# Seven-product feed-forward turns: two down units in every turn, a tail of short and long units, and low-half terms last in the first turn

## The chip, the core and the metric

The kernel runs on one NeuronCore of a Trainium2 chip. The metric is the device time of one execution in microseconds (us). TensorE (PE in the profile) multiplies, VectorE (DVE), ScalarE (ACT) and GpSimd (POOL) prepare its operands and take its results, and SyncE (SP) issues the weight loads.

## The reference

Two transformer-like blocks are computed on 528 tokens (16 learned ones and 512 inputs; the last stages keep only 512). The first has two layers, each with a feed-forward part, a mixer and a second feed-forward part; the second block has one layer and ends in a feed-forward part. What matters here is the feed-forward part:

```python
def swiglu(x, w_gu, w_down):
    gate, up = jnp.split(x @ w_gu, 2, axis=-1)
    return (jax.nn.silu(gate) * up) @ w_down
...
        h = h + 0.5 * swiglu(rms_norm(h, ffn1_norm[l]), ffn1_w_gu[l], ffn1_w_down[l])
...
        h = h + 0.5 * swiglu(rms_norm(h, ffn2_norm[l]), ffn2_w_gu[l], ffn2_w_down[l])
...
        x = x + (jax.nn.silu(h2 @ w_ffn_gate[l]) * (h2 @ w_ffn_up[l])) @ w_ffn_down[l]
```

Rows of `x` have 1024 numbers (8 tiles of 128, `KD`) and the hidden width is 2816 (22 tiles, `FT`). All of it is float32.

## The kernel before, in words

**Numbers in two halves.** Each float32 operand is held as a high part (`xh`, `wh`, `ah`) and a low part (`xl`, `wl`, `al`), and a product is the sum of three terms: high by high, low tokens by high weights, high tokens by low weights. For weights, ACT writes `wh` from the loaded `raw` (`hi`, line 1312) and POOL writes `wl = raw - wh` (`split`, line 586; `split_half`, line 598, for one half of a unit). A term with `wl` can't start before POOL is done.

**Units.** PE works through a list of units, one 128-column block of a weight matrix each, with 2 to 8 row tiles. Unit k uses slot k mod 4 of `raw`, `wh` and `wl`. SP loads unit k once PE has finished unit k-4. Results of plain units go to PSUM `pair[k mod 2]`; PE may start unit k only when the result of unit k-2 has been read (the semaphore `evacuated`).

**Feed-forward stages.** Four of the five feed-forward parts run in the form `ffn_w`. They are called A (layer 0, first), B (layer 0, second), C (layer 1, first) and D (second block, 512 tokens) here. Each computes 4 hidden tiles with plain units (8 units) and the other 18 in 18 **turns**, t = 0 to 17. A turn computes gate and up of one hidden tile with seven products (a Strassen-like scheme with combined weights `SH`/`SL` and combined tokens `TH`/`TL`) of 12 matmuls each, into the four banks of `aux`. In the code a turn is `turn` in each engine's block; the products are issued by `product` (line 790). DVE adds the products up (lines 1940, 1948, 1951, 1956), ACT applies silu, and DVE ends the tile by writing its low part `al` (line 1924), which raises `a_ready`.

**Down units.** The down projection needs finished hidden tiles. Inside a turn, after the fourth and after the last product, PE runs a down unit with four row tiles (`BLOCK`, 24 matmuls at 528 tokens) of an earlier group of hidden tiles; DVE adds its result to `hT` (`add_residual`, line 1848). `DOWNS` says how many a turn has: 2 in turns 0 to 14, 1 in turns 15 and 16, none in turn 17; that is 32 units, 4 groups by 8 column blocks. After a turn without its second down unit the next turn's first product would need `aux` bank 3 at once, so turns 16 and 17 put it into a bank of `pair` (`own_pair`, `first_bank`), and turn 17 moves its gate product one place later.

**The tail.** After turn 17 come 8 down units of six row tiles (`W_TAIL`, hidden tiles 16 to 21; 36 matmuls each), m = 0 to 7. Units 0 and 1 are interleaved by row tile (with one matmul group of each last), because hidden tile 21 comes late. In stages A, B and C the result of each tail unit goes through `residual`: DVE adds it to `hT` (line 1848), ACT squares it and writes `xh` (lines 1325, 1326), then `wh` of unit m+3 (line 1312), and DVE adds the square up and writes `xl` (lines 1837, 1838), all before DVE turns to the next unit's result. The next stage's first unit uses `xh`/`xl` row tile by row tile, and its sum of squares (line 759) needs all eight. In stage D the tail only stores: DVE adds, ACT issues the output DMA (line 1469), and the kernel ends.

Of the kernel before, what the change touches and what calls it, by code (L numbers as in the profile page):

```python
# [27 lines left out]
P = 128  # L28
# [3 lines left out]
KD = D // P  # L32
# [24 lines left out]
PLAIN = 4  # L57
# [79 lines left out]
def build(nc, a, out):  # L137
    with ExitStack() as ctx:
# [209 lines left out]
        def singles():  # L348

            k, m = W_FIRST + 4 * 12, 0  # L350
            for t in range(12, W_PAIRS):
                yield t, k, range(m, m + DOWNS[t])
                k, m = k + 2 + DOWNS[t], m + DOWNS[t]

# [128 lines left out]
        def _(sp):  # L483
# [29 lines left out]
            def ffn_w(l, ub, gate, up, down, up0, hold=False):  # L513
# [7 lines left out]
                for g in range(1, 4):  # L521
# [6 lines left out]
                for t, k, ms in singles():  # L528
                    load(l, ub + k, cols(up, l, 0, KD, up0 + (PLAIN + t) * P), KD)
                    load(l, ub + k + 1, cols(gate, l, 0, KD, (PLAIN + t) * P), KD)  # L530
                    for j, m in enumerate(ms):
                        load(l, ub + k + 2 + j, cols(down, l, 3 * BLOCK, BLOCK, m * P), BLOCK)
# [41 lines left out]
        def _(pool):  # L574
# [34 lines left out]
            def ffn_w(l, ub, fs):  # L609
# [3 lines left out]
                for g in range(1, 4):  # L613
# [4 lines left out]
                run(l, ub + W_END, [W_TAIL] * 4, KD // 4)  # L618
# [88 lines left out]
        def _(pe):  # L707
# [63 lines left out]
            def turn(l, k, n, i, fs, th, xs, a0, nd=2, own=None):  # L771
# [12 lines left out]

                def product(b, w, x, lo=None):
                    for t, (u, y) in enumerate(((w[0], x[0]), (w[0], x[1]), (w[1], x[0]))):
                        if t == 2 and lo is not None:
                            pe.wait_ge(*lo)
                        for kk in range(4):
                            mm = nc.tensor.matmul(b[:, 0:th], u(kk), y(kk), start=t == 0 and kk == 0, stop=t == 2 and kk == 3)  # L790
                    return mm
                up, gate = (wh[:, s, :], wl[:, s, :]), (wh[:, s1, :], wl[:, s1, :])

                pe.wait_ge(S["split_hi"], U(l, k, i) + 1)
                if own is not None:
                    pe.wait_ge(S["evacuated"], U(l, k - 1) + 1 + PAIRS)
                else:
                    pe.wait_ge(S["w_free"], n + 1)
                product(first_bank(own), weights(*up, 0), tokens(0, 0), (S["split_done"], U(l, k, i) + 1)).then_inc(S["w_prod"], 1)
                if own is not None:  # L800
                    pe.wait_ge(S["w_up"], n * 2 - 1)
                product(aux[:, 2, :], weights(*up, HK4), tokens(4, 0)).then_inc(S["gemm_done"], 1)
                pe.wait_ge(S["w_tlo"], 4 * fs + 4)

                def gate_product():
                    pe.wait_ge(S["split_hi"], U(l, k + 1, i) + 1)
                    product(aux[:, 0, :], weights(*gate, HK4), combined(3), (S["split_done"], U(l, k + 1, i) + 1)).then_inc(S["gemm_done"], 1)
# [4 lines left out]
                if nd:  # L812
                    gemm(l, k + 2, BLOCK, xs, th, i, ready=lambda kk: (S["a_ready"], a0))
                else:
                    gate_product()
# [6 lines left out]
                if own is not None:  # L822
                    pe.wait_ge(S["w_free"], n + 1)
                product(aux[:, 3, :], weights(SH, SL, 1536), tokens(4, 1)).then_inc(S["w_prod"], 1)
                if nd > 1:
                    gemm(l, k + 3, BLOCK, xs, th, i)

            def ffn_w(l, ub, fi, x0, T, nrm, fs):
# [13 lines left out]
                for g in range(1, 4):  # L842
                    with pe.Fori(0, 4) as i:
                        turn(l, ub + W_FIRST + 16 * (g - 1), n0 + 4 * (g - 1) + i, i, fs, th, *block(g - 1))
                for t, k, ms in singles():
                    turn(l, ub + k, n0 + t, 0, fs, th, *block(3), len(ms), own_pair(t, ub))
# [7 lines left out]
                for j in range(2, KD):  # L854
                    gemm(l, k + j, W_TAIL, (ah, al), th)
# [444 lines left out]
        def _(act):  # L1300
# [62 lines left out]
            def turn(l, k, n, i, T, f, tile, nd=2, after=2, own=None):  # L1363

                th = T // 2
                if own is not None:
                    act.wait_ge(S["w_read"], n * 2 - 1)
                act.wait_ge(S["w_prod"], n * 5 + 5 + 1)
                nc.scalar.activation(tm(SQA)[:, 0:th], first_bank(own)[:, 0:th], ACT.Copy).then_inc(S["w_p1"], 1)
                if nd > 1:  # L1370
                    hi(l, k + 3, i, BLOCK * P)
                q = k + 2 + nd
                if after is None:
                    hi(l, q + 1, i, W_TAIL * P)
# [9 lines left out]
                if after is not None:  # L1384
                    hi(l, q + 2, i, (BLOCK if after else W_TAIL) * P)
# [1334 lines left out]
```

## Time and profile before

| what | value |
|---|---|
| median of 3 runs | 3198.28 us (3195.89 to 3201.35) |
| the profiled execution's own time | 3201.69 us |
| its span (first to last instruction in the trace) | 3199.9 us |
| PE busy | 3111.8 us, 97% of the span |
| PE weight loads busy | 2848.1 us, 89% |
| DVE, ACT, POOL busy | 67%, 38%, 42% |
| mean granted TensorE clock | 0.989 of full |

The engine rows give the time in which an engine had an instruction under way. A matmul that waits in PE's pipe counts as busy, so that short gaps of PE don't show in the 97%; starts of consecutive groups show them. A row of the windows view gives a stretch of the trace and its length, then the busy time and the instructions of PE, PE's weight loads, DVE, ACT and POOL, then the mean TensorE clock that was granted (1.00 is full speed), the DMA share and GB/s. A row of the timeline gives start, duration, engine, line, operation, output and inputs, shape and count, and in brackets the idle time before it and what ended it.

### The profile page before, as it was taken

Reading aid. Unit: us, or ns where it says so; the run is one execution under the profiler, and the core shown is the slowest. Engines: PE = TensorE matmul, PEld = TensorE weight load, DVE = VectorE, ACT = ScalarE, POOL = GpSimd, SP = SyncE. Lnnn points to the kernel's source line nnn. Section 1 sums busy time; section 2 is a strip of 40 time slices with the busy share of each in tenths; the row PEclk is TensorE's granted clock in tenths of the full one; section 3 lists DMA queues with packets and bytes.
Section 4 is the critical chain, followed back from the end, with each engine's and each line's share of the span. In section 5 each row is a group of like instructions: output and inputs, shape, how many; then the busy total and the mean of one; then the engine's idle time right before and its main releaser. Section 6 shows DMA issues by size and latency. Waiting matters only on the chain.

```text
span 3199.9 us, 56181 instructions
## 1 busy us (share of the span) xinstructions
PE 3111.8 (97%) x21236; PEld 2848.1 (89%) x21236; DVE 2140.2 (67%) x3071; ACT 1214.0 (38%) x1825; POOL 1353.5 (42%) x960
## 2 busy tenths in 40 slices
PE   8999999999999999999999999999999998999999
PEld 7999988899999999999998888788888786788998
DVE  7888663477588886888763467633234578768885
ACT  5433443322343444444344322332324344344442
POOL 3444442233534444444443233644455563344443
PEclk9999999999999999999999999999999999999999
DMA  4333322233323333333332123333333534233333
GB/s 134 98 95 93 90 74 60 51 90 121 99 86 97 97 104 88 88 97 99 91 82 71 47 79 126 100 97 106 93 97 87 112 97 135 66 95 97 100 101 96
DMA packets 546214, 299.02 MB, mean 93 GB/s; under 512 B 24368, under 2 KB 529840, under 8 KB 545904
## 3 DMA queue, kind: packets, MB, share of 16 engines
q1 hardware_dynamic: 515728, 259.86, 28.7%
q10 hardware_dynamic: 30304, 36.65, 3.6%
q8 instruction: 125, 2.05, 0.3%
q14 instruction: 57, 0.47, 0.0%
HBM read 278.37 MB, written 16.91 MB: 92 GB/s over the span
## 4 chain that ended last, share of the span: by engine, by line
PE 59%; issue 22%; POOL 8%; DVE 7%; DMA 1%; ACT 1%; ACTq 1%; POOLq 0%; DVEq 0%; SPq 0%
PE aux L790 21%; PE pair L725 21%; PE pair L727 15%; POOL wl L586 8%; DMA raw<-ffn_w_gu 1%; DVE R L1909 1%; DVE tmp L1919 1%; ACTq L1702 0%; DVE al L1924 0%; DVE TL L1915 0%; DVE hT L1848 0%; DMA raw<-w_ffn_gate 0%; DVE R L1908 0%; DVE xl L2152 0%; DVE tmp L1824 0%
## 5 line engine op out<-in xcount | busy, mean ns | idle before, releaser
L586 POOL TENSOR_TENSOR wl<-raw,wh 128x256 fp32r<-128x256 f32 (+3 forms) x848 | 1174.8, 1405 | 1816.7 <-ACT wh L1312 1368.6
L1312 ACT ACTIVATE wh<-raw 128x1024 fp32r<-128x1024 f32 (+4 forms) x613 | 511.5, 835 | 481.8 <-DMA raw<-ffn_w_gu 250.5
L1848 DVE SCALAR_TENSOR_TENSOR hT<-pair,hT 128x528 f32 (+3 forms) x208 | 144.7, 695 | 170.7 <-PE pair L725 127.2
L727 PE MATMUL pair<-xh,wh 128*128 128x264 f32 x1344 | 233.6, 296 | 22.5 <-DVE xl L2152 11.1
L725 PE MATMUL pair<-xh,wh 128*128 128x512 f32 x776 | 220.7, 406 | 0.1
L727 PE MATMUL pair<-xl,wh 128*128 128x264 f32 x1344 | 220.7, 286 | 0.0
L727 PEld LDWEIGHTS pair<-xh,wh 128*128 128x128 f32 x1344 | 190.0, 193 | 30.0 <-issue 14.8
L727 PE MATMUL pair<-ah,wh 128*128 128x264 f32 x1256 | 211.8, 286 | 4.9 <-ACT wh L1312 2.9
L727 PE MATMUL pair<-xh,wl 128*128 128x264 f32 x1344 | 215.3, 286 | 0.8 <-POOL wl L586 0.8
L725 PE MATMUL pair<-xl,wh 128*128 128x512 f32 x776 | 212.3, 395 | 0.0
L725 PE MATMUL pair<-xh,wl 128*128 128x512 f32 x776 | 209.2, 395 | 0.3 <-POOL wl L586 0.3
L727 PE MATMUL pair<-al,wh 128*128 128x264 f32 x1256 | 208.9, 283 | 0.0
L727 PE MATMUL pair<-ah,wl 128*128 128x264 f32 x1256 | 191.3, 283 | 0.0
L727 PEld LDWEIGHTS pair<-xl,wh 128*128 128x128 f32 x1344 | 187.6, 190 | 0.1
L727 PEld LDWEIGHTS pair<-xh,wl 128*128 128x128 f32 x1344 | 184.8, 190 | 1.2 <-POOL wl L586 1.2
L727 PEld LDWEIGHTS pair<-ah,wh 128*128 128x128 f32 x1256 | 176.2, 188 | 7.2 <-ACT wh L1312 3.3
L1360 ACT ACTIVATE ah<-tmp 128x528 f32 (+3 forms) x110 | 70.5, 641 | 289.2 <-DVE tmp L1919 289.2
L725 PEld LDWEIGHTS pair<-xh,wh 128*128 128x128 f32 x776 | 145.0, 190 | 36.6 <-issue 4.7
L725 PEld LDWEIGHTS pair<-xh,wl 128*128 128x128 f32 x776 | 146.1, 188 | 34.8 <-POOL wl L586 0.7
L725 PEld LDWEIGHTS pair<-xl,wh 128*128 128x128 f32 x776 | 146.6, 189 | 33.1 <-issue 0.2
L727 PEld LDWEIGHTS pair<-al,wh 128*128 128x128 f32 x1256 | 175.3, 188 | 0.0
L727 PEld LDWEIGHTS pair<-ah,wl 128*128 128x128 f32 x1256 | 168.2, 188 | 0.0
(429 smaller groups left out, 6671.8 us busy)
## 6 DMA issues: line engine op xcount, KB each, us to landing
raw<-ffn_w_gu SPq DMA_DIRECT2D x176, 512.0 KB, 3.9
raw<-w_in SPq DMA_DIRECT2D x103, 512.0 KB, 3.9
raw<-ffn_w_down SPq DMA_DIRECT2D x96, 256.0 KB, 2.8
raw<-ffn_w_down SPq DMA_DIRECT2D x32, 384.0 KB, 3.4
raw<-w_out SPq DMA_DIRECT2D x24, 512.0 KB, 3.8
raw<-w_ffn_gate SPq DMA_DIRECT2D x22, 512.0 KB, 4.6
raw<-w_ffn_up SPq DMA_DIRECT2D x22, 512.0 KB, 3.8
gate_scratch<-gst ACTq DMA_DIRECT2D x32, 256.0 KB, 3.1
```

The lines of the kernel that those rows point to most:

```text
L586: ins = nc.gpsimd.tensor_tensor(wl[:, k % SPL, n], raw[:, k % SPL, n], wh[:, k % SPL, n].bitcast(F32), ALU.subtract)
L725: return nc.tensor.matmul(pp[:, 0, :], wk, x[:, kk, t0:t0 + SEQ], start=first, stop=last)
L727: mm = nc.tensor.matmul(pp[:, h, 0:th], wk, x[:, kk, t0 + h * th:t0 + (h + 1) * th], start=first, stop=last)
L790: mm = nc.tensor.matmul(b[:, 0:th], u(kk), y(kk), start=t == 0 and kk == 0, stop=t == 2 and kk == 3)
L1312: nc.scalar.activation(wh[:, k % SPL, n0:n], raw[:, k % SPL, n0:n], ACT.Copy).then_inc(S["split_hi"], 1)
L1360: nc.scalar.activation(ah[:, bass.ds(tile, 1), 0:T].rearrange("p o t -> p (o t)"), tm(A32, T), ACT.Copy).then_inc(S["ahi_done"], 1)
L1848: v.scalar_tensor_tensor(halves(hm, T // 2), psum_pair(k, T // 2), factor, halves(hm, T // 2), ALU.mult, ALU.add).then_inc(S["evacuated"], ...
L1909: step(v.scalar_tensor_tensor(t2, b22, own(kk + 4), t1, ALU.mult, ALU.subtract))
L1919: v.tensor_tensor(tm(A32, T), tm(SG, T), tm(US, T), ALU.mult).then_inc(S["a_done"], 1)
```

## The change

**Down units.** All 18 turns have two down units of four row tiles. The four that are new (in turns 16 and 17) take hidden tiles 16 to 19 for the column blocks m = 2, 4, 6 and 7. Their tail units keep only hidden tiles 20 and 21: two row tiles, 12 matmuls at 528 tokens. The tail is then long, long, short, long, short, long, short, short. The number of matmuls is the same. `own_pair`, `first_bank` and the moved gate product are gone, and turns 12 to 15 are a loop. Each stage has 88 units where it had 84.

**The first turn.** In turn 0 PE issues the two terms with `wh` of its first three products, and only then the terms with `wl` of the three, in order.

```diff
-DOWNS = (2,) * 15 + (1, 1, 0)
-assert len(DOWNS) == W_PAIRS and sum(DOWNS) == 4 * KD
-W_KT = [KD] * (2 * PLAIN) + [x for nd in DOWNS for x in [KD, KD] + [BLOCK] * nd] + [W_TAIL] * KD
+TAIL_SHORT = (2, 4, 6, 7)
+TAIL_KT = tuple(W_TAIL - BLOCK if m in TAIL_SHORT else W_TAIL for m in range(KD))
+W_KT = [KD] * (2 * PLAIN) + [KD, KD, BLOCK, BLOCK] * W_PAIRS + list(TAIL_KT)
...
-                k = ub + W_END
-                with sp.Fori(0, KD // 4) as i:
-                    for j in range(4):
-                        load(l, k + j, cols(down, l, 4 * BLOCK, W_TAIL, j * P + i * (4 * P)), W_TAIL, i)
+                for m, kt in enumerate(TAIL_KT):
+                    load(l, ub + W_END + m, cols(down, l, FT - kt, kt, m * P), kt)
...
+                up_lo, gate_lo = (S["split_done"], U(l, k, i) + 1), (S["split_done"], U(l, k + 1, i) + 1)
 
                 pe.wait_ge(S["split_hi"], U(l, k, i) + 1)
-                if own is not None:
-                    pe.wait_ge(S["evacuated"], U(l, k - 1) + 1 + PAIRS)
+                pe.wait_ge(S["w_free"], n + 1)
+                if first:
+                    main(*p1)
+                    main(*p2)
+                    pe.wait_ge(S["w_tlo"], 4 * fs + 4)
+                    pe.wait_ge(S["split_hi"], U(l, k + 1, i) + 1)
+                    main(*p4)
+                    pe.wait_ge(*up_lo)
+                    rest(*p1).then_inc(S["w_prod"], 1)
+                    rest(*p2).then_inc(S["gemm_done"], 1)
+                    pe.wait_ge(*gate_lo)
+                    rest(*p4).then_inc(S["gemm_done"], 1)
                 else:
...
-                if nd:
-                    gemm(l, k + 2, BLOCK, xs, th, i, ready=lambda kk: (S["a_ready"], a0))
-                else:
-                    gate_product()
+                gemm(l, k + 2, BLOCK, xs, th, i, ready=lambda kk: (S["a_ready"], a0))
...
-                if nd > 1:
-                    gemm(l, k + 3, BLOCK, xs, th, i)
+                gemm(l, k + 3, BLOCK, xs, th, i)
...
                 for j in range(2, KD):
-                    gemm(l, k + j, W_TAIL, (ah, al), th)
+                    o = W_TAIL - TAIL_KT[j]
+                    gemm(l, k + j, TAIL_KT[j], (ah[:, o:W_TAIL, :], al[:, o:W_TAIL, :]), th)
```

Here `main` issues a product's two terms with high weights (line 777 of the changed kernel) and `rest` the term with low weights (line 781). The order of instructions on PE at the head of stage A's turn 0, before:

```order
L790 MATMUL aux<-xh,wh 128x264 x4
L790 MATMUL aux<-xl,wh 128x264 x4
L790 MATMUL aux<-xh,wl 128x264 x4
L790 MATMUL aux<-xh,wh 128x264 x4
L790 MATMUL aux<-xl,wh 128x264 x4
L790 MATMUL aux<-xh,wl 128x264 x4
```

And with the change:

```order
L777 MATMUL aux<-xh,wh 128x264 x4
L777 MATMUL aux<-xl,wh 128x264 x4
L777 MATMUL aux<-xh,wh 128x264 x4
L777 MATMUL aux<-xl,wh 128x264 x4
L777 MATMUL aux<-TH,wh 128x264 x4
L777 MATMUL aux<-TL,wh 128x264 x4
L781 MATMUL aux<-xh,wl 128x264 x8
L781 MATMUL aux<-TH,wl 128x264 x4
L777 MATMUL aux<-TH,SH 128x264 x4
```

The first group with `wl` moved behind 24 matmuls where 8 stood before it. On PE from the middle of stage A's tail into the next stage (units 2 and 3, before):

```order
L727 MATMUL pair<-ah,wh 128x264 x12
L727 MATMUL pair<-al,wh 128x264 x12
L727 MATMUL pair<-ah,wl 128x264 x12
L727 MATMUL pair<-ah,wh 128x264 x12
L727 MATMUL pair<-al,wh 128x264 x12
```

And with the change units 5, 6 and 7 and the head of the next stage (`xh` appears):

```order
L716 MATMUL pair<-ah,wh 128x264 x12
L716 MATMUL pair<-al,wh 128x264 x12
L716 MATMUL pair<-ah,wl 128x264 x12
L716 MATMUL pair<-ah,wh 128x264 x4
L716 MATMUL pair<-al,wh 128x264 x4
L716 MATMUL pair<-ah,wl 128x264 x4
L716 MATMUL pair<-ah,wh 128x264 x4
L716 MATMUL pair<-al,wh 128x264 x4
L716 MATMUL pair<-ah,wl 128x264 x4
L716 MATMUL pair<-xh,wh 128x264 x2
```

Units 6 and 7 have 12 matmuls each where they had 36; ACT, POOL and DVE keep one piece of work for each unit between them, and only its `wh` and `wl` get shorter.

## Rows read from the trace of the kernel before

**Rows 1.** Waits of PE: us in total, times, longest, for two causes.

```profile
PE aux L790 <- POOL wl L586: 9.1, 4, 2.8
PE aux L790 <- DVE tmp L1940: 7.3, 4, 1.9
```

**Rows 2.** Timeline, turn 0 of stage B: start, us, engine, work, [idle before].

```profile
921.03 0.65 PE L790 MATMUL aux<-xh,wh 128*128 128x264 f32 x4
...
923.02 0.61 ACT L1312 ACTIVATE wh<-raw 128x512 fp32r<-128x512 f32 x1
923.98 2.27 POOL L598 TENSOR_TENSOR wl<-raw,wh 128x512 fp32r<-128x512 f32 x1
924.07 0.76 PE L790 MATMUL aux<-xh,wl 128*128 128x264 f32 x4 [1.91 <-POOL wl L586]
...
927.87 0.69 DVE L1924 TENSOR_TENSOR al<-tmp,ah 128x528 fp32r<-128x528 f32 x1
...
930.57 0.40 PE L727 MATMUL pair<-ah,wh 128*128 128x264 f32 x2
```

**Rows 3.** Windows from `al`'s end to turn 0's first down unit (A, C, D).

```profile
74.90:75.38 0.48, 0.48 (x6) 0.48 (x5) 0.00 (x0) 0.24 (x1) 0.48 (x1) 1.00 1.14 346
1297.40:1299.43 2.03, 2.03 (x18) 2.03 (x17) 0.00 (x0) 0.23 (x1) 2.03 (x2) 0.99 0.87 242
2891.46:2893.36 1.90, 1.90 (x18) 1.90 (x17) 0.00 (x0) 0.23 (x1) 1.90 (x2) 1.00 0.92 269
```

**Rows 4.** Windows: a turn with two down units, at 528 and 512 tokens.

```profile
299.98:316.00 16.02, 16.02 (x134) 16.02 (x133) 13.95 (x17) 6.47 (x10) 7.19 (x5) 1.00 0.35 99
3107.24:3122.80 15.56, 15.56 (x110) 14.51 (x110) 14.00 (x17) 6.58 (x10) 7.32 (x5) 1.00 0.35 102
```

**Rows 5.** Windows from turn 15's start to the tail's start; stages A to D.

```profile
316.00:356.43 40.43, 38.48 (x302) 38.06 (x301) 32.11 (x40) 14.72 (x21) 17.18 (x10) 0.96 0.35 99
1167.17:1206.39 39.22, 36.94 (x302) 36.52 (x301) 32.50 (x39) 14.94 (x21) 17.18 (x10) 1.00 0.35 102
1535.10:1575.55 40.45, 38.48 (x302) 38.06 (x301) 31.95 (x39) 14.73 (x22) 17.22 (x10) 0.96 0.34 99
3122.80:3162.67 39.87, 37.30 (x277) 35.83 (x276) 32.05 (x39) 14.74 (x21) 17.21 (x10) 0.96 0.35 99
```

**Rows 6.** Windows of three stretches behind a wait of PE (the seventh number: TensorE clock).

```profile
352.00:355.30 3.30, 3.30 (x18) 3.30 (x17) 0.43 (x1) 0.00 (x0) 1.23 (x1) 0.50 0.02 5
925.30:928.50 3.20, 3.20 (x18) 3.20 (x17) 3.17 (x4) 1.66 (x4) 1.36 (x2) 0.51 0.04 10
1202.00:1206.00 4.00, 4.00 (x33) 4.00 (x34) 0.78 (x2) 0.00 (x0) 2.75 (x2) 1.00 0.33 97
```

**Rows 7.** Timeline, stage A's tail: DVE and PE, to the sum of squares.

```profile
364.67 0.71 DVE L1848 SCALAR_TENSOR_TENSOR hT<-pair,hT 128x528 f32<-128x528 f32 x1 [4.29 <-PE pair L727]
365.52 1.69 PE L727 MATMUL pair<-ah,wh 128*128 128x264 f32 x12 [0.16 <-DVE hT L1848]
...
367.74 0.70 DVE L1848 SCALAR_TENSOR_TENSOR hT<-pair,hT 128x528 f32<-128x528 f32 x1
369.94 1.61 PE L727 MATMUL pair<-ah,wh 128*128 128x264 f32 x12
371.09 0.70 DVE L1848 SCALAR_TENSOR_TENSOR hT<-pair,hT 128x528 f32<-128x528 f32 x1
...
374.28 1.61 PE L727 MATMUL pair<-ah,wh 128*128 128x264 f32 x12
374.48 0.71 DVE L1848 SCALAR_TENSOR_TENSOR hT<-pair,hT 128x528 f32<-128x528 f32 x1
...
391.84 0.71 DVE L1848 SCALAR_TENSOR_TENSOR hT<-pair,hT 128x528 f32<-128x528 f32 x1 [0.91 <-PE pair L727]
394.51 0.76 DVE L1838 SCALAR_TENSOR_TENSOR xl<-hT,gcur,xh 128x528 fp32r<-128x528 f32 x1
...
396.76 1.05 PE L759 MATMUL aux<-tmp,con 128*128 128x264 f32 x4
```

More of the change, by code:

```diff
@@ L348, in singles @@
         def singles():
[L350 to L353, printed above, removed]
+            for t in range(16, W_PAIRS):
+                yield t, W_FIRST + 4 * t, TAIL_SHORT[2 * (t - 16):2 * (t - 16) + 2]
         class Plan:
@@ L520, in ffn_w @@
                     load(l, ub + 2 * j + 1, cols(up, l, 0, KD, up0 + j * P), KD)
-                for g in range(1, 4):
+                for g in range(1, 5):
                     k = ub + W_FIRST + 16 * (g - 1)
@@ L612, in ffn_w @@
                 n0 = W_PAIRS * fs
-                for g in range(1, 4):
+                for g in range(1, 5):
                     with pool.Fori(0, 4) as i:
@@ L617, in ffn_w @@
                     turn(l, ub + k, n0 + t, 0, len(ms))
-                run(l, ub + W_END, [W_TAIL] * 4, KD // 4)
+                for m, kt in enumerate(TAIL_KT):
+                    split(l, ub + W_END + m, kt)
             def ffn(l, ub, beside):
@@ L769, in norm_sum_2, with turn @@
                 mm.then_inc(S["ss_done"], 1)
-            def turn(l, k, n, i, fs, th, xs, a0, nd=2, own=None):
+            def turn(l, k, n, i, fs, th, xs, a0, first=False):
                 s, s1 = k % SPL, (k + 1) % SPL
@@ L783, in combined, with main @@
                     return [lambda kk, x=x: x[:, m, kk, :] for x in (wth(th), wtl(th))]
-                def product(b, w, x, lo=None):
[L786 to L791, printed above, removed]
+                def main(b, w, x):
+                    for t, y in enumerate(x):
+                        for kk in range(4):
+                            nc.tensor.matmul(b[:, 0:th], w[0](kk), y(kk), start=t == 0 and kk == 0, stop=False)
@@ L792, in turn, with rest @@
+                def rest(b, w, x):
+                    for kk in range(4):
+                        mm = nc.tensor.matmul(b[:, 0:th], w[1](kk), x[0](kk), start=False, stop=kk == 3)
+                    return mm
+                def product(b, w, x, lo=None):
+                    main(b, w, x)
+                    if lo is not None:
+                        pe.wait_ge(*lo)
+                    return rest(b, w, x)
                 up, gate = (wh[:, s, :], wl[:, s, :]), (wh[:, s1, :], wl[:, s1, :])
+                p1, p2, p4 = ((aux[:, 3, :], weights(*up, 0), tokens(0, 0)), (aux[:, 2, :], weights(*up, HK4), tokens(4, 0)),
+                              (aux[:, 0, :], weights(*gate, HK4), combined(3)))
@@ L802, in turn @@
-                product(aux[:, 2, :], weights(*up, HK4), tokens(4, 0)).then_inc(S["gemm_done"], 1)
-                pe.wait_ge(S["w_tlo"], 4 * fs + 4)
-                def gate_product():
+                pe.wait_ge(S["w_free"], n + 1)
[10 more added lines that the diff above has]
+                    rest(*p4).then_inc(S["gemm_done"], 1)
+                else:
+                    product(*p1, up_lo).then_inc(S["w_prod"], 1)
+                    product(*p2).then_inc(S["gemm_done"], 1)
@@ L806, in gate_product @@
                     pe.wait_ge(S["split_hi"], U(l, k + 1, i) + 1)
[L807 to L809 removed]
+                    product(*p4, gate_lo).then_inc(S["gemm_done"], 1)
                 pe.wait_ge(S["w_hi"], n * 2 + 1)
                 product(aux[:, 1, :], weights(SH, SL, 512), combined(1), (S["w_lo"], n * 2 + 1)).then_inc(S["w_prod"], 1)
[L812 to L815 removed]
+                gemm(l, k + 2, BLOCK, xs, th, i, ready=lambda kk: (S["a_ready"], a0))
@@ L841, in block @@
                     return (ah[:, o:o + BLOCK, :], al[:, o:o + BLOCK, :]), fi * FT + BLOCK * (g + 1)
-                for g in range(1, 4):
+                turn(l, ub + W_FIRST, n0, 0, fs, th, *block(0), first=True)
+                with pe.Fori(0, 3) as i:
+                    turn(l, ub + W_FIRST + 4, n0 + 1 + i, i, fs, th, *block(0))
+                for g in range(2, 5):
                     with pe.Fori(0, 4) as i:
@@ L1406, in ffn_w @@
                         w_his(n0, 1, n0 * 5 + 5)
-                for g in range(1, 4):
+                for g in range(1, 5):
                     with act.Fori(0, 4) as i:
@@ L1992, in ffn_w @@
                         w_sums(l, ub + W_FIRST, n0, 0)
-                for g in range(1, 4):
+                for g in range(1, 5):
                     with dve.Fori(0, 4) as i:
```

48 lines of the change are left out of this document (15 added, 33 removed).

## The prediction

> **What bounds the kernel now.** I read the waits of PE first, then the timeline of PE to see when equal pieces of work start, then windows. PE is busy for 97% of the span, and nearly all of the rest is a few waits, so time changes only where PE's waits or its clock change. Two kinds of wait lie where the edits are, once in each of the four feed-forward stages [rows 1]: turn 0 waits for POOL's `wl` (9.1 us in four waits, 2.3 each), and turn 17 waits for DVE's reading of `aux` (line 1940; 7.3 us in four, 1.8 each). The number of matmuls doesn't change. The questions are what stands behind each wait once it is gone, and whether the tail, with less PE work per unit, still keeps PE fed.
>
> **Part 1, the low-half terms of turn 0.** The reader should look at stage B [rows 2]. PE starts at 921.03, issues 8 matmuls, and at 922.0 stands until POOL's `wl` is there at 924.07. With the change it goes on with the high terms of the second product until 922.97 (a turn's 132 matmuls in 16.02 us [rows 4] give 0.121 us each, 0.97 for 8). The third product needs ACT's `wh` of the gate unit, which ends at 923.63; its 8 high matmuls end at 924.65. Eight low matmuls of the up unit: 925.6. The gate's `wl` ends at 926.25; four matmuls: 926.8. Product four (12 matmuls): 928.25. Then stands the down unit, which waits for `a_ready` of the last plain tile: 927.87 + 0.69 = 928.56. That chain on DVE and ACT doesn't hang on PE, so it doesn't move. PE starts the down unit at about 928.6 instead of 930.57: 1.97 us won. The end of `al` is thus the floor in every stage. It lies 0.48, 2.01, 2.03 and 1.90 us ahead of the down unit in A, B, C and D [rows 2, 3], less 0.05 each for waking: **-6.2 us**. The waits that take the old one's place (0.7 for `wh`, 0.7 for the gate's `wl`, 0.35 for `al`) make up most of the old one; in B, C and D a good part of the gain is instead the clock that fell behind the old wait [rows 6]. What moves with PE (SP's loads behind units k and k+1, DVE's reading behind product four) comes earlier, none of it later.
>
> **Part 2, turns 15 to 17.** A turn with two down units takes 16.02 us, at 512 tokens 15.56, with no wait inside [rows 4]. Three take 48.06 (D: 46.68). Before, the three took 40.43, 39.22, 40.45 and 39.87 us [rows 5], the waits and slow clocks of turn 17 included. So they get longer by 7.6, 8.8, 7.6 and 6.8: +30.9 us. Four down units of 24 matmuls are 4 x 24 x 0.121 = 11.6 us of work; what is missing to that (4.0 in A, 2.8 in B) is what the change wins at turn 17. I take no wait for turns 15 to 17: down units stand between the last product and the next first one as in turn 14.
>
> **Part 3, the tail of stages A, B and C.** Here the trace shows the change's price. One tail unit takes 374.28 less 369.94 = 4.34 us on PE [rows 7]; a short one takes a third, 1.45. But each unit, long or short, has the same chain behind it: DVE's addition 0.7, ACT's square and `xh`, DVE's square sum and `xl`, and only then the next addition. Units 0 and 1 end together, so DVE starts in arrears, and the reader can see its own pace: additions start at 364.67, 367.74, 371.09 and 374.48, that is 3.07, then 3.35 and 3.39 apart [rows 7]. That is less than 4.34, so PE doesn't wait now. It is far more than 1.45. And PE may begin unit m only when unit m-2 has been added. With starts A(m) of the additions at a pace of 3.38 behind the third, and 0.85 us from such a start to PE's (365.52 less 364.67 [rows 7]), in the times of stage A before:
>
> unit 2 runs 365.52 to 366.97; unit 3 waits for A(1) + 0.85 = 368.6, to 372.9; unit 4, to 374.4; unit 5 waits for A(3) + 0.85 = 375.3, to 379.7; unit 6, to 381.1; unit 7 waits for A(5) + 0.85 = 381.23 + 0.85 = 382.1, to 383.5; the next stage's first unit waits for A(6) + 0.85 = 385.5.
>
> A(7) is 388.0. From an addition's start to the end of its `xl` it is 394.51 + 0.76 - 391.84 = 3.43 [rows 7], so the sum of squares can start at 391.5. Before it started at 396.76. The tail is **5.3 us** shorter, where PE's work is 11.6 us shorter; five new waits (1.6, 0.9, 1.0, 1.9 and about 1.0 at the end) eat the rest. Three stages: -15.8 us.
>
> **Part 4, the tail of stage D.** There ACT only stores, and one DVE operation a unit follows. PE stays the bound: a long unit is about 4.2 us (4.34 by the ratio of 15.56 to 16.02), four short ones save 4 x 2.8 = 11.2. The last two outputs follow each other by 1.4 us instead of 4.2, for which I give 0.3 (bounds 0 and 1.4, all of the time between them): -10.9 us. The weights' loads: a short unit's is a third of the bytes, and the load of unit m waits for unit m-4 as before, two long units back at least; I cost it at nothing, hidden under these. Four more units a stage cost SP, ACT and POOL four more commands, under PE's 16 us turns.
>
> **Sum.** -6.2 + 30.9 - 15.8 - 10.9 = -2.0 us, if the clock stays at full speed at all the new waits.
>
> **The clock.** Behind a wait the granted clock is at times half (1.2 instead of 2.4 GHz): 0.50 for over 3 us behind turn 17's wait in stage A, 0.51 behind turn 0's in B; behind the same wait of 1.8 us in stage B's turn 17 it stayed at 1.00 [rows 6]. Such a fall costs 3.3 x 0.5 = 1.65 us of PE. The new tail has 2.9 us of waits in its last 6 us, and in turn 0 1.8 us are split into three. In the tail the falls that lie before the last two waits are hidden by them; one behind the wait before the next stage, or at the sum of squares, is not. In turn 0 about 0.6 to 1.1 is left of it, since the wait for `al` takes some. I take half of these: half of three tails at 1.7 and of four first turns at 0.9, 4.3 us. Bounds: none, and two falls in each tail with one in each turn 0, 3 x 3.3 + 4 x 1.1 = 14 us. The sum is then +2.3. The profiled execution took 3201.7, so its like would be 3204.0; the median is 3.4 lower at 3198.28, and the same +2.3 gives **3200.5 us**.
>
> The Trainium skill ("TensorE: Matmul & The Clock Gate", section "A second HAM failure mode: psum-queue depth-cycling") says that a PE which idles briefly between groups of matmuls often enough makes its clock oscillate, and that throughput suffers between the bursts. By that rule the clock would fall in every new tail, which is the second case below; the traces so far bear it out in part, with a fall behind one of two equal waits.
>
> **The rivals.** First, the likeliest case, near balance: chance 0.67, from 3194 to 3205.
>
> Second, slower by the clock: falls in all three tails, in some twice. For it speaks that the tail's waits come in a row; against it that stage B's 1.8 us brought none. From five falls' worth (8.4 us, that is -2.0 + 8.4 = +6.4) it decides the sign; it ends at 3205 to 3210. Chance 0.15.
>
> Third, turn 0 wins nothing, because POOL and ACT are asked for the same pieces in another order and PE's second and third wait grow: the edit does not do what it says. Then the sum is +4.2 and with the clock +8.5: 3206.8. Against it speaks that `al`'s end and POOL's end don't depend on PE. Chance 0.07.
>
> Fourth, the tail's chain doesn't bind, because ACT's shorter `wh` and POOL's shorter `wl` let DVE go faster or the additions overlap. The tails would save 11.6 each: -2.0 - 3 x 6.3 = -20.9, 3177. Against it: in the arrears of [rows 7] ACT and DVE wait for each other, not for POOL. Chance 0.05; another 0.06 for what I don't see (loads that come late, +-10).
>
> About 0.2% (6.4 us) is what a measurement of this kernel can tell from no change. Faster by more than that needs the fourth case or most of the unseen: 0.06. Slower takes nearly all of the second, most of the third: 0.2. No change: 0.74. The range for 8 in 10 is 3193 to 3208: below it lies the fourth case, above it the clock's worst.
>
> **What would show each step.** In the changed profile: turn 0's waits of PE for `wl` near 0.7 us instead of 2.3, and one for `al`; no wait of PE of over 1 us inside turn 17; additions (line 1848) 3.35 to 3.4 apart through all of the tail in A, B and C, and PE waiting for them four times; sum of squares 35.0 us behind the tail's start where it was 396.76 - 356.43 = 40.3; stage D's end 4 us earlier behind turn 15's start. The prediction is wrong if additions come closer than 3.3, if the down unit of turn 0 starts well behind `al`, or if windows of the tails show the clock at half for much of them.

## The result and the profile after

The changed kernel takes 3205.42 us (median of 9 runs, 3197.7 to 3208.92), the kernel before 3198.28 in the same series. The ratio is 1.002, with an interval of 1.0011 to 1.0028: 6.4 us slower, 3.5 to 9 (the two medians lie 7.1 apart). That touches the 0.2% from which a difference could be told; the forecast was 3200.5 in a range of 3193 to 3208.

The profiled execution took 3207.92 us, its span is 3206.1 (before 3199.9) and its mean granted clock 0.991. The engine row of the page and three rows of PE's waits (us in total, times, longest):

```profile
PE 3105.3 (97%) x21236; PEld 2839.4 (89%) x21236; DVE 2172.9 (68%) x3087; ACT 1217.7 (38%) x1841; POOL 1359.3 (42%) x976
...
PE pair L716 <- DVE hT L1842: 14.7, 13, 1.8
PE aux L777 <- DVE tmp L1949: 6.3, 7, 1.9
PE aux L777 <- ACT wh L1312: 4.6, 4, 1.6
```

The 9.1 us for `wl` in turn 0 and the 7.3 us in turn 17 [rows 1] are gone. In their place stand 4.6 us for ACT's `wh` in turn 0 and 14.7 us for DVE's additions in the tails, which the prediction had named. The 6.3 us at line 1949, the reading of `aux` bank 3, are in turns 1 to 14; the same instruction (line 1956) cost PE 4.0 us before.

**Turn 0.** PE's timeline of stage B after, to be held beside [rows 2]:

```profile
925.11 0.65 PE L777 MATMUL aux<-xh,wh 128*128 128x264 f32 x4
...
927.88 0.72 PE L777 MATMUL aux<-TH,wh 128*128 128x264 f32 x4 [0.65 <-ACT wh L1312]
...
930.41 0.76 PE L781 MATMUL aux<-TH,wl 128*128 128x264 f32 x4 [0.36 <-POOL wl L586]
...
932.83 0.48 PE L716 MATMUL pair<-ah,wh 128*128 128x264 f32 x2 [0.19 <-DVE al L1918]
```

The wait of 1.91 has become three of 0.65, 0.36 and 0.19 (0.7, 0.7 and 0.35 were forecast), and PE reaches the down unit 7.72 us behind its start instead of 9.54. The last of the three is for `al`: the floor that was forecast.

**Turns 15 to 17.** Windows from turn 15's start to the tail's start, stages A to D, the same stretches as [rows 5]:

```profile
315.49:363.58 48.09, 48.09 (x398) 48.09 (x397) 40.55 (x46) 17.52 (x27) 21.62 (x13) 1.00 0.31 91
1172.97:1221.05 48.08, 48.08 (x398) 48.08 (x397) 39.06 (x46) 17.42 (x26) 21.70 (x13) 1.00 0.31 91
1543.51:1591.59 48.08, 48.08 (x398) 48.08 (x397) 40.07 (x46) 17.56 (x26) 20.66 (x13) 1.00 0.32 91
3133.03:3180.07 47.04, 46.98 (x326) 43.23 (x326) 40.26 (x46) 17.33 (x26) 21.62 (x13) 1.00 0.32 93
```

PE doesn't wait there at all. **The tail of stage A**, DVE's additions (line 1842) and `xl` (line 1832), POOL's `wl` (line 574) and PE's waits, then the windows of the tails of A and B from their start to the sum of squares (C's is the same):

```profile
374.22 0.76 DVE L1832 SCALAR_TENSOR_TENSOR xl<-hT,gcur,xh 128x528 fp32r<-128x528 f32 x1
374.90 0.70 DVE L1842 SCALAR_TENSOR_TENSOR hT<-pair,hT 128x528 f32<-128x528 f32 x1
375.74 1.69 PE L716 MATMUL pair<-ah,wh 128*128 128x264 f32 x12 [1.39 <-DVE hT L1842]
377.29 0.95 POOL L574 TENSOR_TENSOR wl<-raw,wh 128x256 fp32r<-128x256 f32 x1 [0.62 <-ACT wh L1312]
377.57 1.25 DVE L1832 SCALAR_TENSOR_TENSOR xl<-hT,gcur,xh 128x528 fp32r<-128x528 f32 x1
378.73 0.70 DVE L1842 SCALAR_TENSOR_TENSOR hT<-pair,hT 128x528 f32<-128x528 f32 x1
...
381.40 0.76 DVE L1832 SCALAR_TENSOR_TENSOR xl<-hT,gcur,xh 128x528 fp32r<-128x528 f32 x1
381.55 2.29 POOL L574 TENSOR_TENSOR wl<-raw,wh 128x768 fp32r<-128x768 f32 x1 [3.31 <-ACT wh L1312]
382.07 0.70 DVE L1842 SCALAR_TENSOR_TENSOR hT<-pair,hT 128x528 f32<-128x528 f32 x1
382.92 1.69 PE L716 MATMUL pair<-ah,wh 128*128 128x264 f32 x12 [1.15 <-DVE hT L1842]
...
390.57 0.73 PE L716 MATMUL pair<-ah,wh 128*128 128x264 f32 x4 [1.62 <-DVE hT L1842]
394.02 0.48 PE L716 MATMUL pair<-xh,wh 128*128 128x264 f32 x2 [1.75 <-DVE hT L1842]
400.29 1.13 PE L748 MATMUL aux<-tmp,con 128*128 128x264 f32 x4 [0.92 <-DVE xl L1832]
```

```profile
363.58:400.29 36.71, 29.71 (x237) 28.61 (x235) 18.93 (x26) 17.10 (x27) 14.44 (x9) 1.00 0.32 91
1221.05:1257.76 36.71, 29.73 (x237) 28.63 (x235) 18.93 (x26) 17.09 (x27) 14.46 (x9) 1.00 0.31 90
```

The tails are 3.6 us shorter than before (40.3), not 5.3, and the clock is at full speed throughout. From 374.90 to 378.73 the additions are 3.83 us apart, where the forecast had 3.35: `xl` took 1.25 instead of 0.76, beside a short `wl` that POOL had begun at 377.29. At 381.40 DVE began first; `xl` took 0.76 and POOL's `wl` 2.29. Three of the eight `xl` in each tail are slow so.

**Where the time went**, in us, after less before, from these starts in the two profiles (turn 0: in A the start of its down unit, in B to D the length of the turn):

| | A | B | C | D | sum | forecast |
|---|---|---|---|---|---|---|
| turn 0 | -0.3 | -1.8 | -1.8 | -1.7 | -5.6 | -6.2 |
| turns 1 to 14 | -0.3 | +3.5 | -0.9 | +0.1 | +2.4 | 0 |
| turns 15 to 17 | +7.7 | +8.9 | +7.6 | +7.2 | +31.3 | +30.9 |
| tail | -3.6 | -3.7 | -3.7 | -11.2 | -22.2 | -26.7 |
| clock, new falls | 0 | 0 | 0 | 0 | 0 | +4.3 |

The sum is +5.9 of the span's +6.2. The last row counts falls in turn 0 and in the tails; turns 1 to 14 hold falls of their own (below). To be explained are the 4.5 us that the tails lack, the clock, and turns 1 to 14.

### The profile page after: what moved, and what is told of

It reads as the page before. It is cut to its first block, busy times and chain, and to the rows that moved or that the text cites. A ratio compares the mean times of both kernels' runs of the same rounds, so it can differ in the third digit from the quotient of the medians.

```text
span 3206.1 us, 56885 instructions
## 1 busy us (share of the span) xinstructions
PE 3105.3 (97%) x21236; PEld 2839.4 (89%) x21236; DVE 2172.9 (68%) x3087; ACT 1217.7 (38%) x1841; POOL 1359.3 (42%) x976
## 4 chain that ended last, share of the span: by engine, by line
PE 57%; issue 22%; DVE 8%; POOL 8%; ACT 2%; DMA 2%; ACTq 1%; POOLq 0%; DVEq 0%; SPq 0%
PE pair L714 21%; PE aux L777 14%; PE pair L716 13%; POOL wl L574 8%; PE aux L781 7%; DMA raw<-ffn_w_gu 1%; DVE hT L1842 1%; DVE R L1903 1%; DVE xl L1832 1%; DVE tmp L1913 1%; ACTq L1696 0%; DVE tmp L1831 0%; ACT tmp L1325 0%; ACT xh L1326 0%; DVE al L1918 0%
## 5 line engine op out<-in xcount | busy, mean ns | idle before, releaser
L1842 DVE SCALAR_TENSOR_TENSOR hT<-pair,hT 128x528 f32 (+3 forms) x224 | 156.0, 696 | 164.0 <-PE pair L714 119.3
L714 PEld LDWEIGHTS pair<-xl,wh 128*128 128x128 f32 x776 | 146.6, 189 | 33.1 <-issue 0.2
```

What stands on the lines that cost most here:

```text
L714: return nc.tensor.matmul(pp[:, 0, :], wk, x[:, kk, t0:t0 + SEQ], start=first, stop=last)
L1842: v.scalar_tensor_tensor(halves(hm, T // 2), psum_pair(k, T // 2), factor, halves(hm, T // 2), ALU.mult, ALU.add).then_inc(S["evacuated"], ...
```

## The experiments

Ratios are to the kernel before, timed in the same series. From each trace I read the same stretches as above.

**The first turn alone.** The kernel before, with only the new order of turn 0:

```diff
+                if first:
+                    main(*p1)
+                    main(*p2)
...
+                    main(*p4)
+                    pe.wait_ge(*up_lo)
+                    rest(*p1).then_inc(S["w_prod"], 1)
+                    rest(*p2).then_inc(S["gemm_done"], 1)
+                    pe.wait_ge(*gate_lo)
+                    rest(*p4).then_inc(S["gemm_done"], 1)
```

> The kernel before with the changed order of turn 0 alone. The two traces put turn 0 at -0.3, -1.8, -1.9 and -1.7 us in stages A to D. If the parts add up, this kernel takes 5.7 us less than before: about 3192.6 us, ratio 0.998. The rival, that the early products of turn 0 only move waits into the following turns (the changed kernel's stage B had two turns of 18 us where 16 is usual), gives no gain: 3198 us.

3188.84 us, ratio 0.9978 (0.9966 to 0.9989): 7 us faster, 3.5 to 11. PE's waits and the window behind turn 17's wait in stage A:

```profile
PE aux L788 <- DVE tmp L1965: 7.3, 4, 1.8
...
PE aux L792 <- POOL wl L598: 1.5, 4, 0.4
```

```profile
346.80:350.10 3.30, 3.30 (x30) 3.30 (x29) 1.52 (x3) 0.00 (x0) 1.27 (x1) 1.00 0.02 5
```

Turn 0 gives its 5.7 us: PE starts the down unit 0.15 us behind `al`'s end in all four stages. The wait of 1.8 us in turn 17 is as before, four times; but the clock behind it is 1.00 in every stage here, and turns 15 to 17 take 38.4 to 39.0 us, where the kernel before took 39.9 to 40.5 in A, C and D [rows 5]. That is worth a look of its own, below.

**The down units alone.** The changed kernel with the old order of turn 0:

```diff
-                turn(l, ub + W_FIRST, n0, 0, fs, th, *block(0), first=True)
+                turn(l, ub + W_FIRST, n0, 0, fs, th, *block(0))
```

> The changed kernel with the order of turn 0 as before. The two traces put turns 15 to 17 at +31.3 us over the four stages and the tails at -22.2 us. If the parts add up, this kernel takes 9.1 us more than before: about 3207.4 us, and some 6 us more than the changed kernel if that is measured fairly at 3205.4 (then 3211). The rival, that turn 0's new order costs what the changed kernel is slower by, gives 3198 us or less here.

3210.06 us, ratio 1.0041 (1.0025 to 1.0056). Turns 15 to 17 are 48.08 us in A to C, 46.66 in D, the tails 37.1, 36.7 and 36.7. So the two parts of the change add up within the intervals (0.9978 times 1.0041 is 1.0019): one wins about 7 us, the other loses some 13. Stage A's tail is the longer one because the clock fell there, behind PE's last wait of 1.76 us:

```profile
390.41:393.71 3.30, 3.30 (x16) 3.30 (x16) 2.14 (x3) 2.04 (x4) 2.59 (x2) 0.50 0.41 121
```

**GpSimd's short `wl` later.** In the tails of A to C ACT writes each short unit's `wh` twice, so that POOL's `wl` starts 0.3 us later:

```diff
                     prep(hT[:, m, T1 - T:T1], gain(m), xh[:, m, 0:T], T)
+                    kts, q = KT2 if l is None else KT1[l] + W_KT[:AHEAD], ub + m + AHEAD
+                    if kts[q] == W_TAIL - BLOCK:
+                        act.wait_ge(raw_loaded[q % SPL], landed(l, q, 0))
+                        nc.scalar.activation(wh[:, q % SPL, BLOCK * P:W_TAIL * P], raw[:, q % SPL, 0:kts[q] * P], ACT.Copy)
                     ahead(l, ub + m)
```

> The changed kernel with one more ACT copy of 256 columns ahead of the wh of each short tail unit in stages A to C, so that POOL's wl starts about 0.4 us later, as behind a long unit. Theory: DVE's xl operation took 1.25 instead of 0.76 us at three units of each tail because POOL's short wl had begun just before it and held what both need; started later, POOL waits for DVE instead. Then all xl operations take 0.76 us, additions come 3.35 apart, and each tail is 1.5 us shorter: 4.4 us less than the changed kernel, 3201 us. The rival, that the operation is slow for a reason of its own (the shorter units bring DVE's work beside other traffic), leaves 3205 us and 1.25 us operations.

3205.86 us, ratio 1.002 (1.0011 to 1.0029): nothing won. Timeline of DVE's `xl` and POOL's `wl` in stage A, and a window behind the last waits of stage B's tail:

```profile
375.90 0.76 DVE L1836 SCALAR_TENSOR_TENSOR xl<-hT,gcur,xh 128x528 fp32r<-128x528 f32 x1
375.94 1.33 POOL L574 TENSOR_TENSOR wl<-raw,wh 128x256 fp32r<-128x256 f32 x1 [0.93 <-ACT wh L1312]
...
382.59 1.33 DVE L1836 SCALAR_TENSOR_TENSOR xl<-hT,gcur,xh 128x528 fp32r<-128x528 f32 x1
382.62 0.73 POOL L574 TENSOR_TENSOR wl<-raw,wh 128x256 fp32r<-128x256 f32 x1 [0.93 <-ACT wh L1312]
```

```profile
1244.00:1247.30 3.30, 1.99 (x11) 1.72 (x10) 2.00 (x3) 2.18 (x4) 2.16 (x1) 0.52 0.60 177
```

The delay only made a near tie: POOL's recorded start is 0.04 or 0.03 us behind DVE's, and in the first pair DVE goes first, in the second POOL; over the three tails POOL does in eight of nine. One of the two takes its own time (0.76 or 0.73), the other 1.33, nearly its time and the first's together. In B and C the clock fell to half behind a wait of 1.8 us, and the tails took 37.8 us.

**GpSimd behind `xl`.** The order made sure of, in the changed kernel: in the tails of A to C POOL's `wl` of short unit m also waits for the `xl` of tile m-3.

```diff
                 for m, kt in enumerate(TAIL_KT):
+                    if t0 is not None and kt < W_TAIL and m >= AHEAD:
+                        pool.wait_ge(S["x_ready"], t0 + m - AHEAD + 1)
                     split(l, ub + W_END + m, kt)
```

> The changed kernel, where GpSimd's wl of the short units 4, 6 and 7 in the tails of A to C also waits for VectorE's xl of the tile three before, so that it cannot begin beside it. Theory (GpSimd's short wl, begun first, holds VectorE's xl up by 0.5 us three times a tail): the three xl take 0.76 us instead of 1.25, all additions 3.3 to 3.4 us apart, tails 35.2 to 35.5 instead of 36.7, total 3200 to 3202. Rival (the xl is slow for another reason, its own operands): xl stay at 1.25 and the total at 3205.

```profile
381.24 0.70 DVE L1844 SCALAR_TENSOR_TENSOR hT<-pair,hT 128x528 f32<-128x528 f32 x1
381.40 0.74 POOL L574 TENSOR_TENSOR wl<-raw,wh 128x256 fp32r<-128x256 f32 x1 [1.74 <-DVE xl L1834]
...
384.59 0.70 DVE L1844 SCALAR_TENSOR_TENSOR hT<-pair,hT 128x528 f32<-128x528 f32 x1
391.27 0.70 DVE L1844 SCALAR_TENSOR_TENSOR hT<-pair,hT 128x528 f32<-128x528 f32 x1
```

All eight `xl` take 0.76, the additions are 3.34 to 3.35 us apart through the middle of the tail, POOL's short `wl` beside an addition takes its 0.74, and the tails take 35.27, 35.25 and 35.27 us. The changed kernel's 36.7 less three times 0.49 is 35.2. With that the cause of 1.4 of the 1.7 us that each tail lacks is shown. The time doesn't show it: 3207.3 us, ratio 1.0019 (1.0009 to 1.0028). The profiled execution took 3215.21, and its turns 1 to 14 were 11 us longer than the changed kernel's, more than the 4.3 us that its tails won.

**The chain broken up.** The changed kernel, where DVE adds unit m+1 before it ends tile m, with two buffers for the squares:

```diff
+                def tile(m):
+                    if m:
+                        dve.wait_ge(S["x_ready"], t0 + m)
+                    prep(t0 + m, hT[:, m, T1 - T:T1], gain(m), xh[:, m, 0:T], xl[:, m, 0:T], T, m == 0, SQ2[m % 2])
                 for m in range(KD):
                     add_residual(l, ub + m, m, factor, T)
-                    prep(t0 + m, hT[:, m, T1 - T:T1], gain(m), xh[:, m, 0:T], xl[:, m, 0:T], T, m == 0)
+                    if m:
+                        tile(m - 1)
+                tile(KD - 1)
```

> The changed kernel with DVE's work in the residual step reordered: it adds unit m+1 before it writes xl of unit m, with two buffers for the square. Theory: the chain of addition, ACT's two passes and DVE's two passes, one unit at a time, is what keeps PE waiting in the tails of A, B and C. With the additions ahead PE's waits in the tails go, each tail is nearly 11.6 us shorter than before's instead of 3.7, and the kernel takes 24 us less than the changed one: about 3181 us. The rival, that short units would wait anyway for their weights (load, wh, wl), gives waits of PE for ACT or POOL in the tails and at most 5 us less: 3200 us.

3198.72 us, ratio 1.0004 (0.9995 to 1.0014); tails 34.65, 34.64 and 34.90. The expected 24 us didn't come. PE's waits of over 0.6 us inside the tail are gone, but at the tail's end stands the timeline

```profile
387.69 2.46 POOL L574 TENSOR_TENSOR wl<-raw,wh 128x1024 fp32r<-128x1024 f32 x1 [3.67 <-ACT wh L1312]
387.80 2.90 DVE L1832 SCALAR_TENSOR_TENSOR xl<-hT,gcur,xh 128x528 fp32r<-128x528 f32 x1
...
394.21 2.77 DVE L1831 TENSOR_TENSOR tmp<-tmp 128x528 f32<-128x528 f32 x1
394.23 0.51 PE L716 MATMUL pair<-xh,wh 128*128 128x264 f32 x2 [2.71 <-DVE xl L1832]
```

DVE's operations of 0.7 us take 2.3 to 2.9, each beside one of POOL's 1024-column `wl` for the next stage, and behind PE's wait of 2.71 us the clock was 0.50 for 3.3 us, in all three tails. The same edit in **the kernel before**:

> The kernel before, its turns and tails untouched, with the one edit of the pipelined variant (VectorE adds unit m+1 before it makes xl of unit m, squares in two buffers). Theory (the chain of addition, ScalarE, xl binds only once the tail has short units): tails of A to C stay at 40.3 us from tail start to sum of squares, within 0.5, total 3194 to 3199. Rival (the order of VectorE's work is worth something in itself, also in the attention's residual): 2 us or more less than before.

3200.42 us, ratio 0.9998 (0.9989 to 1.0007), tails of 40.4: no gain, since PE's 4.34 us a unit bounds that tail. The chain binds only with short units.

**Short units early.** The changed kernel, then the one with the chain broken up, with

```diff
-TAIL_SHORT = (2, 4, 6, 7)
+TAIL_SHORT = (2, 3, 4, 5)
```

> The changed kernel with the four short units at 2, 3, 4, 5 instead of 2, 4, 6, 7, everything else equal. Theory (the tail is bound by the chain through VectorE and ScalarE at 3.4 to 3.5 us a unit, whatever TensorE has to do): the sum of squares stays within 0.7 us of 36.7 in A to C, PE only waits in other places, total within 3 us of the changed kernel in A to C; stage D's tail has no such chain and may end later, since its last unit is then long: up to 3 us more. Rival (PE's waits behind units 6 and 7 are what costs, and long units at the end would cover them): tails of 33 to 34.5, total 6 to 9 us less.

3212.67 us, ratio 1.0039 (1.0026 to 1.0052), tails of A to C 37.6, 0.9 longer than the changed kernel's where 0.7 at most was expected; stage D's is 0.9 longer too. PE's waits stand in other places, and the last addition starts 33.1 us behind the tail's start as before (33.0): the chain runs on whatever PE has to do. The sum of squares comes later because PE, with two long units at the end, gets to it only 0.9 us after the last `xl`. These tails are 3.4 us of the loss against the changed kernel; the rest of the 6 us between the two ratios isn't explained.

> The pipelined variant with the short units at 2, 3, 4, 5. In the pipelined one the gain was lost at the end of the tail, where VectorE's xl and additions of the last units wait for GpSimd's 1024-column wl of the next stage while PE has only short units left. Theory: with long units 6 and 7 at the end PE has 8.7 us of work over that stretch, the half clock behind it disappears, tails 31 to 33.5 instead of 34.7, total 3189 to 3196. Rival (the chain simply ends when GpSimd's three long wl are through): tails stay at 34 to 35, total 3197 to 3201.

3201.39 us, ratio 1.0003 (0.9993 to 1.0012), tails 33.48, 33.48 and 33.50. The tails are at the upper end of what was hoped, the total isn't; in this profile turns 1 to 14 were 6.5 us longer than in the changed kernel's.

**Every `wl` behind `xl`.** The last kernel, where in the tails of A to C POOL's `wl` of tail units 3 to 7 and of the next stage's first three units waits for the `xl` of the tile three before:

```diff
+                    if t0 is not None and m >= AHEAD:
+                        pool.wait_ge(S["x_ready"], t0 + m - AHEAD + 1)
```

> The pipelined variant with the short units at 2, 3, 4, 5, where in the tails of A to C every wl of GpSimd, of the tail's later units and of the next stage's first three, waits for VectorE's xl of the tile three before. Theory (in the last third of the tail VectorE's sum of squares takes 2.3 to 2.8 us instead of 0.71 because GpSimd's 1024-column wl began first; with the order turned round GpSimd pays): sums of squares at 0.71, tails of 31 to 32 us instead of 33.5, ratio to before 0.9975 to 0.999. Rival (GpSimd is then late with the next stage's wl and PE waits there instead): tails 31 to 32 but as much idle behind them, ratio 1.000.

```profile
387.71 2.40 POOL L574 TENSOR_TENSOR wl<-raw,wh 128x1024 fp32r<-128x1024 f32 x1 [1.32 <-DVE xl L1839]
389.59 0.71 DVE L1849 SCALAR_TENSOR_TENSOR hT<-pair,hT 128x528 f32<-128x528 f32 x1 [1.95 <-PE pair L723]
390.21 0.70 DVE L1838 TENSOR_TENSOR tmp<-tmp 128x528 f32<-128x528 f32 x1
391.67 2.40 POOL L574 TENSOR_TENSOR wl<-raw,wh 128x1024 fp32r<-128x1024 f32 x1 [1.55 <-DVE xl L1839]
391.70 2.93 DVE L1838 TENSOR_TENSOR tmp<-tmp 128x528 f32<-128x528 f32 x1
```

```profile
363.73:395.46 31.73, 29.68 (x237) 28.62 (x235) 21.19 (x26) 17.51 (x27) 11.90 (x9) 1.00 0.37 105
```

3194.54 us, ratio 0.9989 (0.9979 to 0.9999): the best with two down units in every turn. Tails are 31.7 us, of which PE is busy for 29.68; two blocked additions of the square are left, one of 1.96 us beside a 768-column `wl` and the one of 2.93. It doesn't beat the first turn alone (0.9978), though the two intervals overlap.

**The same kernels again**, one profile each, of before and of the changed kernel.

> The kernel before once more, for a second profile of the same code. Theory (the half clock behind the last long turn's 1.8 us wait in stages A and C, some 3 us in all, and the excess of turns 1 to 14, 12 us over their shortest pace, are of that one execution and not of the kernel): in this profile the half clock is in other stages or none, and the excess of turns 1 to 14 is another number between 7 and 20 us. Rival (they belong to the code): the same turns show them again.

> The changed kernel once more. Theory: turn 0, turns 15 to 17 and the tails come out within 0.5 us of the first profile in every stage, the excess of turns 1 to 14 does not (14.5 us there; between 7 and 26 here). Rival: turns 4, 8, 9 and 12 are late again by the same amounts.

The kernel before took 3200.9 us. Windows behind turn 17's wait (1.80 to 1.86 us in every stage), A, C, B and D:

```profile
352.30:355.60 3.30, 3.30 (x29) 3.30 (x28) 1.47 (x3) 0.00 (x0) 1.29 (x1) 1.00 0.02 5
1569.70:1573.00 3.30, 3.30 (x19) 3.30 (x19) 0.00 (x0) 0.00 (x0) 1.35 (x1) 0.60 0.00 0
1202.00:1205.30 3.30, 3.30 (x30) 3.30 (x29) 1.54 (x3) 0.00 (x0) 1.22 (x1) 1.00 0.02 6
3157.50:3160.80 3.30, 3.30 (x22) 3.30 (x22) 0.09 (x1) 0.00 (x0) 1.34 (x1) 0.69 0.00 0
```

Stage A, at half clock in [rows 6], is at full clock here, with the same wait; C and D are low again. So whether this fall comes is decided by the execution and not by the code alone. The profile from which I forecast had it in three stages, some 1.5 us each (40.45 less 38.95), this one in two, the kernels with the first turn alone and with only the chain broken up in none: 5 of 16 stages. Turn 0 differs more: in its old order the clock fell in 10 of 16 stages (four profiles), behind waits of 1.9 to 2.8 us, in the new order in none of 40 (ten profiles), behind waits of 0.6 to 1.6. The changed kernel took 3207.17; its turns 15 to 17 (48.08, 48.08, 48.26, 46.96) and tails (36.69, 36.71, 36.70) repeat to 0.2 us, and turns 12 of A (16.98 us) and 8 of A (18.26) are late again; turn 9 of A (17.89 in the first profile, 16.24 here) and turn 5 of B (17.66, 16.13) are not. These two had the clock at half for 3.4 us each, behind a wait for the late turn ahead of them.

**Turns 12 to 15 written out.** The changed kernel, with these four turns unrolled on every engine as in the kernel before, where the change had made a fourth loop of them (SP's, POOL's, ACT's and DVE's line shown; PE's is `range(2, 4)`):

```diff
-                for g in range(1, 5):
+                for g in range(1, 4):
```

> The changed kernel with turns 12 to 15 written out one by one on every engine, as in the kernel before, instead of as a fourth loop; same work, same order. It asks whether the excess of turns 1 to 14 over their shortest pace (16 us on average over nine profiles with 88 units a stage, 11 over four with 84) has to do with that loop. Theory (it comes from loads that land late by chance, the loop has no part in it): excess between 9 and 26 us, total within 3 us of the changed kernel, ratio to before 1.001 to 1.003. Rival (the loop's start costs, on SyncE's queue or in fetched instructions): turn 12 no longer late, excess 8 to 12 us, ratio 0.9995 to 1.001.

3203.01 us, ratio 1.0005 (0.9996 to 1.0014), where the changed kernel has 1.002 (1.0011 to 1.0028). Stage A's turn 12 in the changed kernel and here:

```profile
266.01:283.33 17.32, 16.30 (x133) 16.08 (x132) 14.15 (x17) 6.43 (x10) 7.13 (x5) 1.00 0.32 92
```

```profile
266.20:282.22 16.02, 16.02 (x134) 16.02 (x133) 13.99 (x17) 6.43 (x9) 7.14 (x5) 1.00 0.34 100
```

In nine profiles with that loop, stage A's turn 12 took 16.1 to 17.3 us, 16.9 on average, and over 16.5 in eight; in five profiles with it written out 16.02, 16.03, 16.09, 16.12 and, once, 18.01. The excess of turns 1 to 14 over their shortest pace (16.02 us, in D 15.5) is 10.6 us here, 9 to 26 with the loop (16.1 on average), 7.4 to 14.3 in the four profiles of kernels with one-down turns. The rival with the loop's start is the better supported one, but it isn't shown: the two intervals overlap, the profile of before has turn 12 late though it is written out, and the difference of 4.8 us between the ratios is more than turn 12 of stage A alone accounts for. The clock fell in this kernel too behind the last wait of stage A's tail (1.77 us), which took 37.15.

A form in which the last four turns have one down unit each, so that only two tail units would be short, wasn't tried: turn 17's down unit would read hidden tile 12 from the slot into which tile 20 is written.

## Why the prediction came out as it did

**Part 1, turn 0: right.** -5.6 against -6.2. The floor at `al` holds in all four stages; PE starts 0.14 to 0.15 us behind `al`'s end, where 0.05 was taken, which is 0.4 of the difference. The rival in which turn 0 wins nothing is refuted by the first turn alone, 0.9978.

**Part 2, turns 15 to 17: right as a difference of the two profiles** (+31.3 against +30.9). But "the waits and slow clocks of turn 17 included" took as the kernel's what was partly one execution's: at full clock the old turns take 38.9 us (D: 38.4), and the change then costs 9.1 to 9.2 in A to C and 8.3 in D, about 36. By that the loss at full clock is some 4.5 us larger than that profile's. Over the four profiles with the old turns 15 to 17 they take 157.3 us on average, and the changed kernel's two have 191.3 and 191.4: some +34.

**Part 3, tails A to C: the mechanism right, the size wrong.** The chain sets the end, with PE's five waits where they were forecast: 1.39, 1.15, 1.62, 1.75 and 0.92 against 1.6, 0.9, 1.0, 1.9 and about 1.0. The wait before unit 7 is the one that grew. The term mis-sized is "additions at a pace of 3.38": three of the intervals are 3.83, since ACT's shorter `wh` (256 columns) let POOL's `wl` begin ahead of DVE's `xl`, which then took 1.25 us instead of 0.76. The sum of squares came 36.7 us behind the tail's start instead of 35.1 (391.5 less 356.43); with POOL held back it came at 35.3. The fourth rival had the same cause in mind with the sign reversed: a faster POOL and ACT would let DVE go faster. They slowed it.

**Part 4, the tail of D: right**, -11.2 against -10.9.

**The clock: mis-sized.** No new tail and no new turn 0 of the changed kernel's two profiles lost clock, behind waits of up to 1.77 us. But the same tail lost it in stage A of two other kernels, the down units alone and the one with turns 12 to 15 written out, behind the last wait of 1.76 and 1.77: 2 of 12 such tails. There it cost 0.45 us (37.15 against 36.7), not the 1.7 that the prediction charged behind this wait, since most of it went into the wait before the sum of squares. A kernel with the same tail but a later `wl` lost it in two of three, behind 1.80, and the one with its short units early in A and B, behind 1.91 and 1.89 (hidden, as the prediction said: 37.6 with and without it). In turn 0 it never came. The +4.3 thus didn't occur, and nearly balanced the tails' +4.8. The second rival, slower by the clock, put the time at 3205 to 3210; the measured 3205.42 lies there, but its condition, falls in all three tails, didn't occur, so that is chance. The Trainium skill's rule on micro-idling ("TensorE: Matmul & The Clock Gate", section "A second HAM failure mode: psum-queue depth-cycling") was not borne out in the changed kernel's tails, with four waits of over 1 us in each and the clock at 1.00.

**Turns 1 to 14: not in the sum at all.** They gave +2.4 us in these profiles. The diff also turned four written-out turns into a loop, for which the prediction has no term. Written out again the kernel is at 1.0005 instead of 1.002, so a part of the 6.4 us, perhaps most of it, may lie there; how much isn't shown.

The forecast of +2.2 in the medians was 4.2 us short. That the time came out slightly slower, and inside the range, is partly luck: errors of 4 to 5 us stood against each other.

What stays open: why a loop's first turn is late. Turns 4 and 8 are the first of their loops in all kernels; in stage A they took over 16.5 us in 9 and in 12 of the fourteen profiles, but in stage C turn 8 never did. Where I looked, the trace shows weights that land late, as in the changed kernel's turn 8 of stage A (18.12 us):

```profile
201.09 1.93 SPq L478 DMA_DIRECT2D raw<-ffn_w_gu  x2
...
209.72 0.69 DVE L1881 TENSOR_TENSOR gst<-raw 128x512 f32<-128x512 f32 x1 [3.89 <-DMA raw<-ffn_w_gu]
...
215.85 1.21 PE L777 MATMUL aux<-xh,wh 128*128 128x264 f32 x4 [1.94 <-DVE tmp L1949]
```

The loads were issued 16.03 us behind the last turn's, as always; DVE waited 3.89 us for them instead of the 1.5 to 1.8 of turns 5 to 7, and PE, behind DVE's combined weights and sums, 1.94. Whether instruction fetches delay them was not told apart.

## What to carry to other kernels

Before work is moved to shorten the bottleneck engine's pieces, look for the per-piece chain behind them: here 11.6 us less of PE's work in a tail was worth 3.6, and the four down units cost 9.1 elsewhere at full clock. When an operation gets shorter, ask whom it now gets ahead of: POOL's `wl` overtook DVE's `xl`, and a plain wait that restored the order won back 1.4 us a tail. Before a wait's cost is read from one profile, see whether another execution of the same code shows the same clock behind it; and of two edits in one change, time each: the small one alone won 7 us.

## What the hardware showed that I had not expected

- **DVE and POOL hold each other up for nearly a whole operation.** `xl` (two SBUF inputs) takes 0.76 us alone and 1.25 beside a 256-column `wl` that began first, up to 2.90 beside a 1024-column one; a 256-column `wl` takes 0.74 undisturbed and 1.33 when `xl` began first. DVE's additions, with one input in PSUM, take 0.70 us in both cases (at 381.24 beside POOL's 0.74). The Trainium skill says the same ("SBUF — State Buffer", section "SBUF: two separate sides"): the port pair that both use is an exclusive lock, and the operation that starts first holds it to its end. This trace agrees, to within 0.2 us: the `xl` that took 1.25 ended 0.58 us behind the end of POOL's `wl` (378.82 and 378.24), where it takes 0.76 alone. Recorded starts 0.03 us apart don't tell who was first.
- **Equal waits, unequal clocks.** Behind the same wait of 1.8 us in the same turn of the same kernel the granted clock was 0.50 in one execution and 1.00 in the next. Cutting turn 0's one wait of 1.9 to 2.8 us into shorter ones took the fall away in all 40 stages looked at.
- **A loop's first turn** was up to 2.5 us longer than its shortest ones (18.53 against 16.02, turn 8 of stage A); in the one read closely, weights had landed late.
